# Two transformer blocks on one core: five small changes of order and of weight tiles in the first block

## The reference

```python
h = rms_norm(x, norm_mix)
proj = h @ w_in                       # q, k, v, gates of all four mixers
y_nsa = nsa_mixer(...)                # k_slc, v_slc, k_win, v_win, gate_logits, rope at positions
y_sb = stick_breaking_mixer(sb_q, sb_k, sb_v)
y_gla = gla_mixer(...)                # each head scaled by rsqrt(mean(o * o))
y_fox = forgetting_mixer(...)         # scores + cumsum(log_sigmoid(f_logit + b_f))
branch = jnp.einsum('bsnc,ncd->bsnd', ys, w_branch)
mixed = jnp.sum(gates * branch, axis=2)
x = x + mixed @ w_out
h2 = rms_norm(x, norm_ff)
return x + jnp.square(jax.nn.relu(h2 @ w_ff1)) @ w_ff2
```

## Time and profile before

| | us |
|---|---|
| median of 3 runs | 2391.42 |
| lowest, highest | 2387.23, 2392.53 |
| profiled execution, its own time | 2388.02 |
| its span | 2386.2 |
| TensorE busy | 2243.0 (94% of the span) |
| VectorE, ScalarE, GpSimd busy | 1231.7, 689.7, 473.1 |
| mean granted clock of TensorE, share of full | 0.975 |

### The profile page before, as it was taken

How to read it: one execution, slowest core, us unless ns; L and a number is a source line. 1 busy time by engine, 2 the same in 40 slices (tenths; PEclk the granted TensorE clock), 3 DMA queues, 4 the chain that set the end, 5 groups by cost and what they waited for, 6 DMA issues and landing times.

```text
span 2386.2 us, 33113 instructions
## 1 busy us (share of the span) xinstructions
PE 2243.0 (94%) x13927; PEld 1811.0 (76%) x13927; DVE 1231.7 (52%) x1670; ACT 689.7 (29%) x1529; POOL 473.1 (20%) x259
## 2 busy tenths in 40 slices
PE   7999999989989999998999898889999998998998
PEld 6898778889888978787998544447888884555887
DVE  5575435764445844367643227562443443465566
ACT  2214453122012144431220367422112113261211
POOL 2221112243312211122432000101111100102332
PEclk9999999999999999999999998989999999998999
DMA  7534665565365356655556210022223222302551
GB/s 227 213 110 153 234 240 162 183 229 194 125 181 213 107 189 217 230 165 217 202 188 227 94 60 18 1 88 71 98 79 106 95 58 93 106 1 91 179 199 61
DMA packets 210048, 340.11 MB, mean 143 GB/s; under 512 B 46451, under 2 KB 78126, under 8 KB 209774
## 3 DMA queue, kind: packets, MB, share of 16 engines
q1 hardware_dynamic: 208808, 334.48, 40.3%
q0 software_dynamic: 944, 3.47, 0.4%
q10 hardware_dynamic: 150, 0.04, 0.0%
HBM read 335.88 MB, written 2.10 MB: 142 GB/s over the span
## 4 chain that ended last, share of the span: by engine, by line
PE 56%; DVE 5%; ACT 3%; issue 1%; DVEq 0%; ACTq 0%
PE bank L2039 15%; PE bank L266 12%; PE bank L268 12%; PE bank L267 12%; PE bank L626 3%; PE bank L2042 1%; ACT work L2359 1%; DVE ring_low L254 1%; ACT work L2275 1%; ACT work L1081 1%; DVE cos L2533 1%; PE bank L629 0%; DVE work L2442 0%; DVE cos L2458 0%; ACT L1081 0%
## 5 line engine op out<-in xcount | busy, mean ns | idle before, releaser
L267 PE MATMUL bank<-hT_high,ring_low 128*128 128x256 f32 (+1 forms) x2032 | 606.6, 299 | 0.0
L267 PEld LDWEIGHTS bank<-hT_high,ring_low 128*128 128x128 f32 x2032 | 390.3, 192 | 12.4 <-issue 0.5
L247 POOL CAST ring_high<-ring 128x2048 fp32r<-128x2048 f32 (+2 forms) x108 | 203.2, 1882 | 718.6 <-PE bank L268 654.0
L254 DVE TENSOR_TENSOR ring_low<-ring,ring_high 128x2048 fp32r<-128x2048 f32 (+2 forms) x108 | 240.3, 2226 | 135.8 <-POOL ring_high L247 135.5
L266 PE MATMUL bank<-hT_low,ring_high 128*128 128x256 f32 (+1 forms) x1008 | 294.9, 293 | 16.2 <-DVE ring_low L254 8.7
L268 PE MATMUL bank<-hT_high,ring_high 128*128 128x256 f32 (+1 forms) x1008 | 287.4, 285 | 0.0
L266 PE MATMUL bank<-ring_low,hidden_high 128*128 128x512 f32 x640 | 254.4, 397 | 0.0
L247 POOL CAST half_high<-ring 128x2048 fp32r<-128x2048 f32 x64 | 125.5, 1965 | 613.8 <-PE bank L268 408.5
L1081 ACT ACTIVATE work<-bank 128x512 f32<-128x512 f32 (+10 forms) x268 | 121.2, 476 | 383.8 <-PE bank L268 325.9
L266 PEld LDWEIGHTS bank<-hT_low,ring_high 128*128 128x128 f32 (+1 forms) x1008 | 192.1, 191 | 27.1 <-issue 19.0
L254 DVE TENSOR_TENSOR ring_low<-ring,half_high 128x2048 fp32r<-128x2048 f32 x64 | 152.8, 2392 | 99.0 <-POOL half_high L247 98.6
(11 more groups left out here) (228 smaller groups left out, 4476.8 us busy)
## 6 DMA issues: line engine op xcount, KB each, us to landing
ring<-w_ff SPq DMA_DIRECT2D x32, 2048.0 KB, 8.1
ring<-mlp_w SPq DMA_DIRECT2D x32, 2048.0 KB, 8.0
ring<-w_in SPq DMA_DIRECT2D x30, 2048.0 KB, 8.3
ring<-w_ada SPq DMA_DIRECT2D x24, 2048.0 KB, 7.6
ring<-w_branch SPq DMA_DIRECT2D x24, 512.0 KB, 6.7
ring<-w_in SPq DMA_DIRECT2D x32, 256.0 KB, 4.2
ring<-w_out SPq DMA_DIRECT2D x4, 2048.0 KB, 7.6
ring<-gqa_w_qkv SPq DMA_DIRECT2D x3, 2048.0 KB, 7.5
```

What stands on the lines that cost most here:

```text
L247: nc.gpsimd.tensor_copy(self.high(i), self.part(i, False)).then_inc(self.high_made, 1)
L254: nc.vector.tensor_tensor(self.part(i, True), self.part(i, False), self.high(i).bitcast(F32), ALU.subtract)\
L267: nc.tensor.matmul(out, a[1], b[0], start=False, stop=False)
```

## The change

Five edits, all in the first block and in the stages that join it to the prologue:

1. The remainders of the feed-forward pieces 0 and 1 are made on DVE ahead of `add_out(1, 0)`, not after `hT_low`.
2. The tiles `kwg` and `kvs` become `kk` (both keys, 256 columns) and `vv` (slc value, win value and gates, 280 columns), two loads each. PE does the slc key before the win key. The number of products is the same.
3. The prologue's angles stand in two parts on DVE, with the remainder of piece 3 (second half of `cmp`) between them.
4. ACT copies the forget row between the statistics of t = 0 and t = 1.
5. In layer 1 the remainder of q1's piece is made after `hT_low`, not before the last sums of layer 0.

```diff
+    kk_tile = ("kk", KD, 2 * P, [((slice(None), slice(None), slice(i * P, i * P + P)),
+                                  w_in[:, :, KS0 + 2 * P * i:KS0 + 2 * P * i + P]) for i in range(2)], done("kskw"))
+    vv_tile = ("vv", KD, P + 152, [((slice(None), slice(None), slice(0, P)), w_in[:, :, KS0 + P:KS0 + 2 * P]),
+                                   ((slice(None), slice(None), slice(P, P + 152)), w_in[:, :, KS0 + 3 * P:KS0 + 3 * P + 152])],
+               done("vwg"))
-    tiles = [*q_tiles, cmp_tile, in_tile("kwg", KS0 + 256, 280, "vwg"), in_tile("kvs", KS0, 256, "vs"),
+    tiles = [*q_tiles, cmp_tile, kk_tile, vv_tile,
...
-    cuts = [("q0", wide[:1], ["q0"]), ("q1", wide[:1], ["q1"]), ("cmp", wide, ["kc", "vc"]), ("kwg", [("n", 0, P)], ["kskw"]),
-            ("kvs", wide[:1], ["vs"]), ("kwg", [("n", P, 152)], ["vwg"]), ("glqk", wide, ["gq", "gk"]),
+    cuts = [("q0", wide[:1], ["q0"]), ("q1", wide[:1], ["q1"]), ("cmp", wide, ["kc", "vc"]), ("kk", wide[:1], ["kskw"]),
+            ("vv", [("n", 0, P), ("n", P, 152)], ["vs", "vwg"]), ("glqk", wide, ["gq", "gk"]),
...
         for t in range(TT):
+            if t == 1:
+                ps = PROJ.arrived(act, "fc")
+                copy(fox_row[0:8, :], ps[0:8, 0:S]).then_inc(PROJ.free("fc"), 1)
             ps = OT.arrived(act, f"go{t}")
...
-        ps = PROJ.arrived(act, "fc")
-        copy(fox_row[0:8, :], ps[0:8, 0:S]).then_inc(PROJ.free("fc"), 1)
...
         if l > 0:
-            Y.make_low(nc, dve, 0, 1)
+            Y.make_low(nc, dve, 0)
         yield
...
             low_bits("xT", ROW_MIX, hT_high[0], c)
-            if l == 0:
+            if l == 0 or c == 1:
                 Y.make_low(nc, dve, c)
...
-        Y.make_low(nc, dve, 2, 3)
+        Y.make_low(nc, dve, 2)
+        yield
+        Y.make_low(nc, dve, 3)
         yield
...
         Y.make_low(nc, dve, OUT_CUT + 3)
+        X.make_low(nc, dve, 0, 1)
         add_out(1, 0)
         norm(0, TT + 1, xn)
         add_out(1, 1)
         norm(1, TT + 2, xn)
         for c in range(2):
             low_bits("yT", ROW_FF, hT_high[1], c)
-        X.make_low(nc, dve, 0, 1, 2, 3)
+        X.make_low(nc, dve, 2, 3)
```

More of the change, by code:

```diff
@@ L711, in tensor @@
         ps = PROJ.claim(pe, "kskw")
-        gemm_T(ps[:, S:2 * S], Y.arrived(pe, "kwg", 0), slice(0, P))
-        w = Y.arrived(pe, "kvs", 0)
-        gemm_T(ps[:, 0:S], w, slice(0, P)).then_inc(PROJ.full, 1)
+        w = Y.arrived(pe, "kk", 0)
+        for i in range(2):
+            last = gemm_T(ps[:, i * S:(i + 1) * S], w, slice(i * P, i * P + P))
+        last.then_inc(PROJ.full, 1)
         ps = PROJ.claim(pe, "vs")
+        w = Y.arrived(pe, "vv", 0)
         for t in range(TT):
-            last = gemm(ps[:, t * P:(t + 1) * P], w, slice(P, 2 * P), t)
+            last = gemm(ps[:, t * P:(t + 1) * P], w, slice(0, P), t)
         last.then_inc(PROJ.full, 1)
-        w = Y.arrived(pe, "kwg", P)
+        w = Y.arrived(pe, "vv", P)
         ps = PROJ.claim(pe, "vwg")
@@ L2719, in build @@
         phases = layers + [second_block(nc, T, dram, out, sem, chip, layers[-1])]
-        stages = [0, 1, 1, 0, 1, 0, 1, 0, 1, 2, 1, 2, 2, 2, 2, 3, 2, 3]
+        stages = [0, 1, 1, 0, 1, 0, 1, 0, 1, 0, 1, 2, 1, 2, 2, 2, 2, 2, 3, 2, 3]
         def run(programs):
```

## The result

The changed kernel's median is **2409.7 us** (2406.54 to 2412.01, 4 runs), beside 2391.35 of the kernel before on the same chip: a ratio of 1.0085, 95% interval 1.0065 to 1.0105. That is +18.4 us where +15.9 was forecast. The profiled execution's span went from 2386.2 to 2407.5 us.

The account below looks back on a forecast made before the run. TensorE's work, idle stretches and lower-clock time bound the kernel. Terms 24.0 - 5.0 - 0.9 - 1.6 - 0.6 = +15.9 us took the profiled execution from 2388.0 to 2403.9; with 3.4 added, median 2407, range 2397 to 2419.

Parts of the forecast that it names:

- Edit 1's wait: VectorE ahead of up0's remainders: stalls until up0's first cast is made, 478.21 + 1.9 = 480.1 in layer 0.
- Edit 1's remainders: VectorE before the third sum: two remainders take 5.66 us, so that sum comes 18.6 us later.
- The chain behind it: From the third sum to the first usable column of hT_low, then in front of up0: 10.7 us.
- clock back: Sum, ada10, transposes, ada11, transposes: 9.0 us if the full clock is back for ada11, 11.4 if not.
- The clock: At up0's products: clock back and full rate costs 9.7 us a layer, half rate throughout 14.5; 12.0 taken.
- Edit 4: At the gates, g1's 2.90 us wait goes and g2 starts earlier: -5.0 us, ends -1.8 and -5.2.
- Edits 2 and 3, layer 0: At layer 0's start, kk lands at 40.4, shortening TensorE's 3.30 us wait: -0.9 us, ends -3.1 and +1.0.
- Edit 2 in layer 1 and edit 5: In layer 1, the wait for the second key goes, -1.6 us; q1's later remainder shortens an idle stretch, -0.6.
- Rival D: Feed-forward: TensorE catches up later, so moving up0's remainders ahead does nothing; -8.1 us, 2383; chance 0.02.
- C: VectorE's wait as computed, but TensorE reaches up0 sooner and all gains are at best ends: +8.2, 2400; chance 0.12.
- B: Clock stays down through up0 and falls at g1 as well: +26.6 us, a median of 2418; chance 0.12.
- Rival A: up0's tile lands before about 459, so up0 starts 6.2 us earlier and keeps the clock: median 2365; chance 0.04.

Follow-up runs that it names:

- casts_held: Changed kernel with one wait more: GpSimd starts up1's casts only when up0's two remainders are cut; 2402.74 us, ratio 1.0053 to the kernel before.
- the first group: Runs taking the edits apart: changed kernel with up0's remainders after hT_low again, 2378.30 us; kernel before with only those remainders moved ahead, 2418.55 us.
- early_slot_one_ahead: Changed kernel with up0 in earlier-freed slot 0, ada11 moved into the feed-forward, only up0's first remainder ahead of the last sums; 2370.67 us, ratio 0.9923.

## Why the prediction was right, and where its steps were off

The forecast 2407 (2397 to 2419) held 2409.7, and the mechanism is the one forecast: edit 1 puts VectorE, and with it TensorE, behind `up0`'s load, and the other edits give back a part. That the sum came within 2.5 us is in part luck. Edit 1 costs 29 to 31 us by the runs, at and past the upper end of its term (+24.0, 19.4 to 29.0), and all else gives 11.0, near its best end, where 8.1 was forecast; the two misses have opposite signs.

- **Edit 1's wait** was right to 0.1 us: the first cast is over 10.4 us after `wo11`'s last matmul, forecast 480.1 - 469.6 = 10.5; `up0` still leaves right behind `wo11`.
- **Edit 1's remainders** is the term that was mis-sized: "VectorE works 5.66 us on the two remainders". They take 7.76, so the third sum moved by 20.6 us against `wo11`, not 18.6. I took the duration from a place where `up0`'s casts end 1.3 us into the pair (there the first takes 3.46 and the second, alone, 2.28) and set it into one where GpSimd casts beside both; casts_held shows that this is the cause.
- **The chain behind it.** Sum to the end of the last transposes: 9.45 us, near the 9.0 of the case "clock back". The step from `hT_low`'s start to `up0` was 2.26 instead of 1.4. Together 12.15, not 10.7.
- **The clock.** Dense products lose 1.7 us a layer to it now (3.4 us at half rate); before, they lost 2.9 in layer 0 and 2.3 in layer 1, where the clock was back at 1138.4. 15.8 - 1.2 = 14.6 and 15.8 - 0.6 = 15.2, where I said 12.0 a layer with 14.5 as the upper end. Two layers make 29.8. The rule of the Trainium skill that I had weighed (TensorE: Matmul & The Clock Gate, part 1) had led to that upper end by way of a chain at half rate throughout. The size came true, the way didn't: `ada11` takes 1.92 us, at full clock. Activity did release the clock, as the Trainium skill says there.
- **Edit 4**: -2.54 us from `g0` to `g2`, forecast -2.5.
- **Edits 2 and 3, layer 0**: -3.36 us, forecast -0.9 with -3.1 as its end. `kk` was there at 39.74, not 40.4; the wait fell to 0.20, and without it no lower clock came over 46 to 49 us, where it had been at half. The price of a lost clock belongs to the wait and goes with it. One term I had put at nothing went the other way: the remainder of piece 3 was to be ready at 36.1, but it started at 35.65 and took 2.29, so `vc` waited 0.64 for it and started 0.9 later. The Trainium skill, DMA: Bandwidth & Descriptors, Specifications, with 512 B as the smallest transfer at line rate, had given 39.9 for `kk`. The trace agrees: its loads went out 0.7 us later than `kwg`'s (32.60 against 31.86) and landed at 39.69, 1,024 KB in 7.1 us, where `kwg`'s 1,120 KB in rows of 1,120 bytes took 8.4.
- **Edit 2 in layer 1 and edit 5**: together -2.2, as forecast; no wait at `kskw`.
- **Missed**: with `glag` there earlier, `gg0` starts after an idle 0.57 instead of 1.06 (0.78 instead of 1.16 in layer 1). I had set the queue's rearrangement at nothing: about -0.9.

The terms as measured sum to 29.8 - 5.1 - 3.4 - 2.2 - 0.9 = +18.2. The profiled spans differ by 21.3; in its second layer the changed one has two short falls of the clock, from 774.0 and from 845.7, that the one before has not, 1.5 us each. What sets these is open. Rival D, that edit 1 does nothing, falls by the first group. C, the short chain, falls by the distances. B had edit 1's size nearly right (14.5 a layer; 14.6 and 15.2 measured) and the rest wrong: edits 2 to 5 came out near or past their best ends, not at B's. Rival A could not happen in this kernel, and its mechanism is what happens once the slot is changed, though at 2376 and 2371 us, not at 2365.

## What to carry to other kernels

An instruction that is moved ahead in an in-order queue brings its wait along: before moving it, look up when its input is there and what stands behind it, and move the load first. Here the same move cost 31 us with the tile late and gave about 5 with the tile early; and of the pair, only the one that the next engine needed first belonged ahead. A duration holds only beside the work that ran with it: where an engine pair shares the stretch, take it from a row where both are busy.

## What the runs showed of the hardware that I had not expected

- VectorE's 128x2048 subtraction takes 2.28 to 2.29 us alone and 3.94 to 3.98 with a GpSimd cast beside it; the cast itself takes 1.90, or up to 3.95 beside a subtraction (the two `late_high` casts: 6.41 us, the two `early_high` ones 3.74). In the changed kernel's rows the one that starts while the other is at work is the slow one, and it ends about its own length after the other's end: cast until 475.39, subtraction until 477.52, cast until 479.28, subtraction until 481.42, cast until 483.17. The norm's product, 0.76 us, takes 1.98 beside a cast.
- In layer 0, 18.6 us of idle time took less from the dense products than 6.4 did: in the changed kernel they ran 3.4 us at half rate, before 5.7, since by then `ada10` and the transposes had run and the clock was back. The rest of the price fell on that thin work: `ada10` took 3.64 us instead of 1.92, the first transposes 1.83 instead of 1.09. The clock fell once more within 1 us of `up0`'s start (0.57 over 494 to 498) after an idle stretch of 1.02 us. In early_slot_one_ahead, after 1.29 us of idle time in both layers, it stayed up in layer 0 and fell for 3.4 us in layer 1 (0.66 over 1114 to 1119). What sets that fall is open.
